# One decoder kernel on one core: the seven weight products of a pair of column blocks in another order, and two of their four weight sums made by accumulating DMAs instead of VectorE

## The chip, the cores and the metric

The kernel runs on one core of one Trainium2 chip. What counts is the device time of one execution in microseconds, the median over runs.

## What is computed

A stack of four layers and one more block over 256 tokens of width 1024, all in float32. Each layer has two feed-forward parts around an attention part; of the reference this is the part that the change touches:

```
def swiglu(x, w13, w2):
    gate, up = jnp.split(x @ w13, 2, axis=-1)
    return (jax.nn.silu(gate) * up) @ w2
...
x = layer_norm(ALPHA * x + 0.5 * swiglu(x, ffn1_w13[i], ffn1_w2[i]), ln_g[i, 0], ln_b[i, 0])
...
x = layer_norm(ALPHA * x + 0.5 * swiglu(x, ffn2_w13[i], ffn2_w2[i]), ln_g[i, 2], ln_b[i, 2])
```

`x` is 256 x 1024, `w13` is 1024 x 5632, `w2` is 2816 x 1024. There are eight such feed-forward parts.

## The kernel before

**Units.** All weights stream from HBM in units of 128 x 2048 floats (1 MB) through a ring of slots. SyncE issues the load of a unit as soon as TensorE has counted the slot's old unit as used (`unit_used`). ScalarE then makes the high part of the unit (`split_hi`, an ACTIVATE `whi<-raw` at L522), VectorE the low part (`split_lo`, a TENSOR_TENSOR `wlo<-raw,whi` at L530, written over `raw`), and each product is three matmuls, high by high, high by low, low by high (`mm3`, L690 to L692). Each engine has its own instruction stream, written out by hand; semaphores join them. An engine that waits holds back all that stands behind in its stream.

**Blocks and pairs.** The hidden width of 2816 is done in 11 blocks of 256 columns (`ffn_order`). A plain block takes two up-units (gate and up columns, each half of the 1024 inputs) and one down-unit. In six of the eight feed-forward parts the blocks 4 and 5, and 8 and 9, are taken as pairs (`PAIRED`), 12 pairs in all. A pair q, q+1 is a 2 x 2 product of blocks done with seven products in place of eight, after Strassen's scheme: sums of weight units (`form_1`, `form_2`, the sum written over `raw`, and `form_2` once more, here called the four weight sums) are multiplied with sums of the rows of x (`rows_s`, split into `rows_h` and `rows_l`), and the products are joined through PSUM banks and four SBUF tiles `term[0]` to `term[3]`.

**Names.** In a pair, v is the unit index of `up(q+1, first half)`, v+1 and v+2 are the two halves of block q, v+3 the second half of block q+1, v+4 and v+5 the down-units of blocks q-1 and q. `before_pair` is VectorE's code during block q-1 and makes the first sums; `paired` is there three times, on ScalarE, VectorE and TensorE, and is the pair itself; `product` is one of the seven products, 12 matmuls of 512 columns. `gate_rows` is the silu times up product of one half of the rows, `gturn` its transposition, `gated_low` and `gated_high` split the result for the down-product `dn`. In the trace the tiles `form_1` and `form_2` are both called `form`, and all `term` tiles `term`. GpSimd works in the feed-forward parts only on the norms around them.

## Time and profile before

| | us |
|---|---|
| median of 3 runs (lowest, highest) | 2476.29 (2475.51, 2476.77) |
| the profiled execution's own time | 2476.37 |
| its span, first to last instruction | 2474.6 |
| TensorE matmul busy | 2423.2 |
| VectorE busy | 1766.0 |
| ScalarE busy | 1255.2 |
| GpSimd busy | 423.4 |

The span is what the rows below are counted in; outside it lie 1.8 us of the profiled execution. The granted TensorE clock was 0.997 of full speed over the span. Busy TensorE is matmuls in flight, so the figure says that something was always in flight, not that the array was at its peak.

### The profile page before, as it was taken

How to read it: one execution, taken by the hardware profiler on the slowest of the kernel's cores; microseconds unless marked ns; L12 is line 12 of the kernel's file. 1: busy time of each engine (PE TensorE's matmuls, PEld its weight loads, DVE VectorE, ACT ScalarE, POOL GpSimd, SP SyncE). 2: the span in 40 equal slices, each digit the busy share in tenths (PEclk: the TensorE clock that was granted, in tenths of full speed). 3: DMA queues.
4: the chain of work that ended last, by engine and by line, in shares of the span. 5: the costliest groups of instructions: out<-in, count | busy, mean ns of one | idle time of the engine just before them, and what ended most of it. 6: DMA issues, size and time to landing. Idle time of an engine off the chain costs nothing. (4 is left out here: it accounts for less than half of the span.)

```text
span 2474.6 us, 32841 instructions
## 1 busy us (share of the span) xinstructions
PE 2423.2 (98%) x13095; PEld 2039.7 (82%) x13095; DVE 1766.0 (71%) x2348; ACT 1255.2 (51%) x1571; POOL 423.4 (17%) x463
## 2 busy tenths in 40 slices
PE   9999999999999999999989999999999998999999
PEld 7888878888888888888877888888878877998998
DVE  5466678778765787787667886887676657897554
ACT  5445555554554555545555555554553455444442
POOL 0002310000001100000231000002359702680000
PEclk9999999999999999999999999999999999999999
DMA  8555445556554455565425555555445542335553
GB/s 269 189 187 157 144 143 191 200 170 197 195 171 137 137 193 198 171 201 191 150 69 180 195 194 179 189 191 169 138 137 187 187 151 89 108 132 202 173 187 111
DMA packets 313944, 418.09 MB, mean 169 GB/s; under 512 B 18761, under 2 KB 271042, under 8 KB 313794
## 3 DMA queue, kind: packets, MB, share of 16 engines
q1 hardware_dynamic: 313794, 416.01, 51.6%
q8 instruction: 105, 1.72, 0.3%
q14 instruction: 45, 0.37, 0.0%
HBM read 414.92 MB, written 1.05 MB: 168 GB/s over the span
## 5 line engine op out<-in xcount | busy, mean ns | idle before, releaser
L530 DVE TENSOR_TENSOR wlo<-raw,whi 128x2048 fp32r<-128x2048 f32 (+1 forms) x388 | 900.5, 2341 | 155.2 <-ACT whi L522 154.5
L522 ACT ACTIVATE whi<-raw 128x2048 fp32r<-128x2048 f32 (+1 forms) x393 | 732.7, 1888 | 6.9 <-DMA raw<-in_ffn_w_dram 4.1
L690 PE MATMUL ps<-whi,xh 128*128 128x512 f32 (+2 forms) x1511 | 566.7, 375 | 7.5 <-DVE wlo L1633 2.2
L692 PE MATMUL ps<-whi,xl 128*128 128x512 f32 (+2 forms) x1511 | 559.5, 370 | 0.0
L691 PE MATMUL ps<-wlo,xh 128*128 128x512 f32 (+2 forms) x1511 | 559.3, 370 | 0.0
L690 PE MATMUL ps<-whi,oh 128*128 128x512 f32 x944 | 380.0, 403 | 0.0
L692 PE MATMUL ps<-whi,ol 128*128 128x512 f32 x944 | 369.1, 391 | 0.0
L691 PE MATMUL ps<-wlo,oh 128*128 128x512 f32 x944 | 367.9, 390 | 0.0
L690 PEld LDWEIGHTS ps<-whi,xh 128*128 128x128 f32 x1511 | 285.0, 189 | 62.0 <-issue 11.5
L692 PEld LDWEIGHTS ps<-whi,xl 128*128 128x128 f32 x1511 | 285.0, 189 | 48.8
L691 PEld LDWEIGHTS ps<-wlo,xh 128*128 128x128 f32 x1511 | 285.3, 189 | 46.4
L877 POOL TENSOR_TENSOR rstd<-ve,mhalf 128x1 f32<-128x1 f32 x26 | 18.8, 724 | 1483.8 <-DVE ve L1577 1302.5
L1076 ACT ACTIVATE sg<-ps 128x256 f32<-128x256 f32 x140 | 53.2, 380 | 321.1 <-PE ps L692 318.9
L1749 DVE TENSOR_TENSOR gt<-sg,ps 128x256 f32<-128x256 f32 x140 | 58.6, 419 | 215.1 <-ACT sg L1076 211.8
L692 PEld LDWEIGHTS ps<-whi,ol 128*128 128x128 f32 x944 | 177.1, 188 | 38.8
L690 PEld LDWEIGHTS ps<-whi,oh 128*128 128x128 f32 x944 | 177.5, 188 | 34.3 <-issue 2.1
L691 PEld LDWEIGHTS ps<-wlo,oh 128*128 128x128 f32 x944 | 177.8, 188 | 32.5
L690 PE MATMUL ps<-xh,whi 128*128 128x256 f32 (+2 forms) x496 | 138.5, 282 | 1.0 <-DVE wlo L530 1.0
L691 PE MATMUL ps<-xl,whi 128*128 128x256 f32 (+2 forms) x496 | 136.1, 277 | 0.0
L692 PE MATMUL ps<-xh,wlo 128*128 128x256 f32 (+2 forms) x496 | 136.0, 277 | 0.0
L1084 ACT ACTIVATE oh<-ps 128x512 fp32r<-128x512 f32 x88 | 52.8, 600 | 120.6 <-PE ps L2433 120.6
L690 PEld LDWEIGHTS ps<-xh,whi 128*128 128x128 f32 (+2 forms) x496 | 91.9, 185 | 3.1 <-DVE wlo L530 1.7
(413 smaller groups left out, 3543.2 us busy)
## 6 DMA issues: line engine op xcount, KB each, us to landing
raw<-in_ffn_w_dram SPq DMA_DIRECT2D x350, 512.0 KB, 4.8
raw<-in_ffn_w_dram SPq DMA_DIRECT2D x88, 1024.0 KB, 5.0
raw<-in_w_ff_dram SPq DMA_DIRECT2D x32, 1024.0 KB, 5.3
raw<-in_w_out_dram SPq DMA_DIRECT2D x20, 1024.0 KB, 4.9
raw<-in_w_in_dram SPq DMA_DIRECT2D x20, 1024.0 KB, 5.1
raw<-in_dsa_w_in_dram SPq DMA_DIRECT2D x32, 512.0 KB, 4.7
raw<-in_dsa_w_in_dram SPq DMA_DIRECT2D x12, 1024.0 KB, 5.1
raw<-in_fox_w_in_dram SPq DMA_DIRECT2D x16, 512.0 KB, 4.8
```

Source lines behind the costliest of these rows:

```text
L522: act.activation(hi(u)[:, 0:w], raw[:, (slot[u] + 1) % SLOTS, 0:w], ACT.Copy).then_inc(sem("hi_ready"), 1)
L530: dve.tensor_tensor(lo(u)[:, 0:w], raw[:, (slot[u] + 1) % SLOTS, 0:w], hi(u)[:, 0:w].bitcast(F32), ALU.subtract).then_inc(sem("lo_ready"), 1)
L690: pe.matmul(o, ah, bh, start=start, stop=False, skip_group_check=True)
L691: pe.matmul(o, ah, bl, start=False, stop=False, skip_group_check=True)
L692: return pe.matmul(o, al, bh, start=False, stop=stop, skip_group_check=True)
L877: pool.tensor_tensor(rstd[:, t, 0:1], ve[:, t, 0:1], mhalf[:, 0:1], ALU.pow).then_inc(sem("rstd_ready"), 1)
L1076: act.activation(sg[:, t, :], src, ACT.Silu).then_inc(sem("silu_done"), 1)
L1084: act.activation(oh[:, c:c + 2, :], ps[:, 6, :].rearrange("p (c s) -> p c s", c=2), ACT.Copy).then_inc(sem("gh_ready"), 1)
L1749: dve.tensor_tensor(gt[:, t, :], sg[:, t, :], up, ALU.mult).then_inc(sem("g_made"), 1)
```

## The change

The seven products are taken in another order and with other signs of the sums, so that four of them (first, third, fifth, seventh) add up in PSUM bank 5 without a reset between, and two (second, fourth) in bank 7. Two of the four weight sums per pair, the one over the raw of unit v+1 and the second one of `form_2`, are no longer made by VectorE but by DMAs with an add that GpSimd issues, from SBUF onto SBUF, 1 MB each. Both later readers (ScalarE's split of v+1, and its `form_high` of the fourth form) wait on the DMAs' semaphores `third_form` and `fourth_form`, VectorE's splits too. ScalarE now keeps four PSUM banks per pair in `term` tiles instead of two; VectorE has three additions of terms instead of five. The used-count of units v+1 and v+2 is given in one step after the fifth product, where it was given after the fourth and the fifth.

```diff
+                if kind == "ffn":
+                    A, D = ffn_units(st)
+                    for n, q in enumerate(st["pairs"]):
+                        v = A(q + 1)
+                        landed(pool, v + 2)
+                        pool.wait_ge(sem("form_made"), b("form_made", 0) + 2 * n + 1)
+                        pool.dma_start(raw_of(v + 1), raw_of(v + 2), accum_op=ALU.add).then_inc(sem("third_form"), 16)
+                        landed(pool, v + 3)
+                        pool.wait_ge(sem("form_lo"), b("form_lo", 0) + 3 * n + 2)
+                        pool.dma_start(form_2[:, :], raw_of(v + 3), accum_op=ALU.add).then_inc(sem("fourth_form"), 16)
...
                     def form_high(n, f, dst, src):
 
-                        act.wait_ge(sem("form_made"), b("form_made", 0) + 4 * n + f)
+                        if f == 3:
+                            act.wait_ge(sem("fourth_form"), b("fourth_form", 0) + 16 * n + 16)
+                        else:
+                            act.wait_ge(sem("form_made"), b("form_made", 0) + 2 * n + f)
                         act.activation(dst[:, :], src[:, :], ACT.Copy).then_inc(sem("form_hi"), 1)
 
+                    def keep(n, k, bank):
+
+                        act.activation(term[k][:, :], ps[:, bank, :], ACT.Copy).then_inc(sem("term_kept"), 1)
+
                     def paired(q):
 
                         n, v = pairs.index(q), A(q + 1)
-                        act.wait_ge(sem("form_made"), b("form_made", 0) + 4 * n + 3)
+                        act.wait_ge(sem("third_form"), b("third_form", 0) + 16 * n + 16)
                         split_hi(act, v + 2)
                         act.wait_ge(sem("unit_used"), v + 1)
-                        act.activation(term[0][:, :], ps[:, 4, :], ACT.Copy).then_inc(sem("term_kept"), 1)
+                        keep(n, 0, 5)
                         split_hi(act, v + 3)
+                        act.wait_ge(sem("form_used"), b("form_used", 0) + 3 * n + 1)
+                        keep(n, 1, 7)
                         act.wait_ge(sem("form_used"), b("form_used", 0) + 3 * n + 2)
-                        act.activation(term[1][:, :], ps[:, 7, :], ACT.Copy).then_inc(sem("term_kept"), 1)
-                        form_high(n, 4, form_4h, form_2)
+                        keep(n, 2, 5)
+                        form_high(n, 3, form_4h, form_2)
                         split_hi(act, v + 4)
+                        act.wait_ge(sem("unit_used"), v + 3)
+                        keep(n, 3, 5)
+                        act.wait_ge(sem("block_made"), b("block_made", 0) + 3 * n + 1)
+                        silu(q, 0, term[2][:, 0:256])
                         act.wait_ge(sem("block_made"), b("block_made", 0) + 3 * n + 2)
-                        silu(q, 0, term[3][:, 0:256])
                         silu(q, 1, term[1][:, 0:256])
                         split_hi(act, v + 5)
-                        act.wait_ge(sem("unit_used"), v + 4)
-                        silu(q + 1, 0, ps[:, 4, 0:256])
                         act.wait_ge(sem("block_made"), b("block_made", 0) + 3 * n + 3)
...
                         if i + 1 in pairs:
                             split_hi(act, A(i + 2))
-                            form_high(pairs.index(i + 1), 2, form_2h, form_2)
+                            form_high(pairs.index(i + 1), 1, form_1h, form_1)
...
                             silu(i, t, ps[:, 4 + t, 0:256])
+                            if t == 0 and i + 1 in pairs:
+                                form_high(pairs.index(i + 1), 2, form_2h, form_2)
...
-                        if i + 1 in pairs:
-                            form_high(pairs.index(i + 1), 1, form_1h, form_1)
-                        elif 0 < i < FIT - 1:
+                        if 0 < i < FIT - 1 and i + 1 not in pairs:
                             split_hi(act, D(i - 1) + ahead[u])
...
-                        ch.link(tt(rows_s[:, 0], first[:, :, r1], second_[:, :, r1], ALU.add))
+                        ch.link(tt(rows_s[:, 0], first[:, :, r1], second_[:, :, r1], ALU.subtract))
...
-                        tt(rows_s[:, 3], second_[:, :, r0], rows_s[:, 1], ALU.subtract).then_inc(sem("rows_made"), 1)
+                        tt(rows_s[:, 3], second_[:, :, r0], rows_s[:, 1], ALU.add).then_inc(sem("rows_made"), 1)
...
-                        n, v, made = pairs.index(q), A(q + 1), b("form_made", 0)
+                        n, v, made = pairs.index(q), A(q + 1), b("form_made", 0) + 2 * pairs.index(q)
                         landed(dve, v)
                         landed(dve, v + 1)
-                        tt(form_1[:, :], raw_of(v + 1), raw_of(v), ALU.subtract).then_inc(sem("form_made"), 1)
+                        tt(form_1[:, :], raw_of(v + 1), raw_of(v), ALU.add).then_inc(sem("form_made"), 1)
                         split_lo(dve, v)
                         landed(dve, v + 2)
-                        dve.wait_ge(sem("form_made"), made + 4 * n + 1)
-                        tt(form_2[:, :], raw_of(v + 2), form_1[:, :], ALU.subtract).then_inc(sem("form_made"), 1)
+                        dve.wait_ge(sem("form_made"), made + 1)
+                        tt(form_2[:, :], raw_of(v + 2), form_1[:, :], ALU.add).then_inc(sem("form_made"), 1)
                         gate_rows(q - 1, 0, ps[:, 4, 256:512])
-                        tt(raw_of(v + 1), raw_of(v + 2), raw_of(v + 1), ALU.subtract).then_inc(sem("form_made"), 1)
+                        form_low(n, 1, form_1l, form_1, form_1h)
                         gate_rows(q - 1, 1, ps[:, 5, 256:512])
-                        form_low(n, 1, form_2l, form_2, form_2h)
-                        form_low(n, 2, form_1l, form_1, form_1h)
+                        form_low(n, 2, form_2l, form_2, form_2h)
                         gated_low(q - 1)
 
                     def paired(q):
 
                         n, v = pairs.index(q), A(q + 1)
-                        kept, sums, blocks, use = (b(name, 0) + k * n for name, k in (("term_kept", 2), ("term_sum", 2), ("block_made", 3), ("form_used", 3)))
+                        kept, use = b("term_kept", 0) + 4 * n, b("form_used", 0) + 3 * n
+                        dve.wait_ge(sem("third_form"), b("third_form", 0) + 16 * n + 16)
                         split_lo(dve, v + 2)
-                        dve.wait_ge(sem("form_used"), use + 1)
-                        dve.wait_ge(sem("term_kept"), kept + 1)
-                        tt(term[0][:, :], term[0][:, :], ps[:, 5, :], ALU.add).then_inc(sem("term_sum"), 1)
-                        landed(dve, v + 3)
-                        tt(form_2[:, :], raw_of(v + 3), form_2[:, :], ALU.subtract).then_inc(sem("form_made"), 1)
+                        dve.wait_ge(sem("fourth_form"), b("fourth_form", 0) + 16 * n + 16)
                         split_lo(dve, v + 3)
-                        dve.wait_ge(sem("unit_used"), v + 2)
-                        dve.wait_ge(sem("term_sum"), sums + 1)
-                        tt(term[2][:, :], term[0][:, :], ps[:, 5, :], ALU.add).then_inc(sem("term_sum"), 1)
                         form_low(n, 3, form_4l, form_2, form_4h)
+                        dve.wait_ge(sem("third_done"), b("third_done", 0) + n + 1)
+                        dve.wait_ge(sem("term_kept"), kept + 3)
+                        tt(term[2][:, :], ps[:, 7, :], term[2][:, :], ALU.subtract).then_inc(sem("block_made"), 1)
                         split_lo(dve, v + 4)
-                        dve.wait_ge(sem("term_kept"), kept + 2)
-                        dve.wait_ge(sem("term_sum"), sums + 2)
-                        tt(term[1][:, :], term[1][:, :], term[2][:, :], ALU.add).then_inc(sem("block_made"), 1)
-                        dve.wait_ge(sem("unit_used"), v + 3)
-                        tt(term[3][:, :], term[0][:, :], ps[:, 7, :], ALU.add).then_inc(sem("block_made"), 1)
-                        dve.wait_ge(sem("block_made"), blocks + 2)
-                        gate_rows(q, 0, term[3][:, 256:512])
+                        dve.wait_ge(sem("term_kept"), kept + 4)
+                        tt(term[1][:, :], term[1][:, :], term[3][:, :], ALU.subtract).then_inc(sem("block_made"), 1)
+                        dve.wait_ge(sem("block_made"), b("block_made", 0) + 3 * n + 2)
+                        gate_rows(q, 0, term[2][:, 256:512])
                         gate_rows(q, 1, term[1][:, 256:512])
+                        dve.wait_ge(sem("unit_used"), v + 4)
+                        tt(term[0][:, :], term[0][:, :], ps[:, 4, :], ALU.add).then_inc(sem("block_made"), 1)
+                        split_lo(dve, v + 5)
+                        dve.wait_ge(sem("block_made"), b("block_made", 0) + 3 * n + 3)
+                        gate_rows(q + 1, 0, term[0][:, 256:512])
                         dve.wait_ge(sem("form_used"), use + 3)
-                        tt(term[2][:, :], term[2][:, :], ps[:, 5, :], ALU.add).then_inc(sem("block_made"), 1)
-                        split_lo(dve, v + 5)
-                        gate_rows(q + 1, 0, ps[:, 4, 256:512])
-                        dve.wait_ge(sem("block_made"), blocks + 3)
-                        gate_rows(q + 1, 1, term[2][:, 256:512])
+                        gate_rows(q + 1, 1, ps[:, 5, 256:512])
                         gated_low(q)
                         split_lo(dve, v + 7)
...
                         n, v = pairs.index(q), A(q + 1)
-                        low, sums, kept = b("form_lo", 0) + 3 * n, b("term_sum", 0) + 2 * n, b("term_kept", 0) + 2 * n
-                        pe.wait_ge(sem("g_made"), b("g_made", 0) + 2 * q - 1)
+                        low, kept = b("form_lo", 0) + 3 * n, b("term_kept", 0) + 4 * n
+                        pe.wait_ge(sem("g_made"), b("g_made", 0) + 2 * q)
                         unit_ready(pe, v)
-                        used(product(4, rows_of(0, 0), hi(v), lo(v), True))
-                        pe.wait_ge(sem("g_made"), b("g_made", 0) + 2 * q)
+                        used(product(5, rows_of(0, 0), hi(v), lo(v), True))
                         pe.wait_ge(sem("rows_lo"), b("rows_lo", 0) + 1)
                         pe.wait_ge(sem("form_lo"), low + 1)
-                        product(5, form_of(1), form_2h, form_2l, True).then_inc(sem("form_used"), 1)
+                        product(7, form_of(0), form_1h, form_1l, True).then_inc(sem("form_used"), 1)
                         pe.wait_ge(sem("form_lo"), low + 2)
-                        product(7, form_of(0), form_1h, form_1l, True).then_inc(sem("form_used"), 1)
-                        unit_ready(pe, v + 1)
-                        pe.wait_ge(sem("term_sum"), sums + 1)
-                        used(product(5, form_of(2), hi(v + 1), lo(v + 1), True))
+                        pe.wait_ge(sem("term_kept"), kept + 1)
+                        product(5, form_of(1), form_2h, form_2l, False).then_inc(sem("form_used"), 1)
                         unit_ready(pe, v + 2)
                         pe.wait_ge(sem("term_kept"), kept + 2)
-                        used(product(7, form_of(3), hi(v + 2), lo(v + 2), False))
+                        product(7, form_of(3), hi(v + 2), lo(v + 2), False).then_inc(sem("third_done"), 1)
+                        pe.wait_ge(sem("term_kept"), kept + 3)
+                        product(5, form_of(2), hi(v + 1), lo(v + 1), False).then_inc(sem("unit_used"), 2)
                         unit_ready(pe, v + 3)
-                        used(product(4, rows_of(1, 0), hi(v + 3), lo(v + 3), False))
+                        used(product(4, rows_of(1, 0), hi(v + 3), lo(v + 3), True))
                         pe.wait_ge(sem("form_lo"), low + 3)
-                        pe.wait_ge(sem("term_sum"), sums + 2)
-                        product(5, rows_of(1, 1), form_4h, form_4l, True).then_inc(sem("form_used"), 1)
+                        pe.wait_ge(sem("term_kept"), kept + 4)
+                        product(5, rows_of(1, 1), form_4h, form_4l, False).then_inc(sem("form_used"), 1)
                         for j in (q, q + 1):
```

In VectorE's stream, from `rows_l` on ahead of the first pair of a feed-forward part (that of pair 4, 5), before the change; a name in brackets is a semaphore that the instruction waits for, `form_54` is `form_1` and `form_57` is `form_2`:

```order
L1787 TENSOR_TENSOR form_57<-raw,form_54 128x2048 [waits form_made,loaded0]
L1749 TENSOR_TENSOR gt<-sg,ps 128x256 [waits gt_done,silu_done]
L1789 TENSOR_TENSOR raw<-raw 128x2048
L1749 TENSOR_TENSOR gt<-sg,ps 128x256 [waits silu_done]
L1761 TENSOR_TENSOR form_2l<-form_57,form_2h 128x2048 [waits form_hi]
L1761 TENSOR_TENSOR form_1l<-form_54,form_1h 128x2048 [waits form_hi]
L1755 TENSOR_TENSOR ol<-ps,oh 128x512 [waits gh_ready]
L530 TENSOR_TENSOR wlo<-raw,whi 128x2048 [waits hi_ready] x2
L1802 TENSOR_TENSOR term_65<-term_65,ps 128x512 [waits term_kept,form_used]
L1804 TENSOR_TENSOR form_57<-raw,form_57 128x2048 [waits loaded1]
L530 TENSOR_TENSOR wlo<-raw,whi 128x2048 [waits hi_ready]
L1808 TENSOR_TENSOR term_67<-term_65,ps 128x512 [waits term_sum,unit_used]
```

The same place after the change (L531 is the old L530, L1784 the old L1761):

```order
L1810 TENSOR_TENSOR form_57<-raw,form_54 128x2048 [waits form_made,loaded0]
L1772 TENSOR_TENSOR gt<-sg,ps 128x256 [waits gt_done,silu_done]
L1784 TENSOR_TENSOR form_1l<-form_54,form_1h 128x2048 [waits form_hi]
L1772 TENSOR_TENSOR gt<-sg,ps 128x256 [waits silu_done]
L1784 TENSOR_TENSOR form_2l<-form_57,form_2h 128x2048 [waits form_hi]
L1778 TENSOR_TENSOR ol<-ps,oh 128x512 [waits gh_ready]
L531 TENSOR_TENSOR wlo<-raw,whi 128x2048 [waits hi_ready,third_form]
L531 TENSOR_TENSOR wlo<-raw,whi 128x2048 [waits hi_ready]
L531 TENSOR_TENSOR wlo<-raw,whi 128x2048 [waits hi_ready,fourth_form]
L1784 TENSOR_TENSOR form_4l<-form_57,form_4h 128x2048 [waits form_hi]
L1828 TENSOR_TENSOR term_67<-ps,term_67 128x512 [waits term_kept,third_done]
```

The two big sums (L1789, L1804) are gone, `form_1l` stands where the first of them stood, and the splits of units v+1 and v+3 have the DMAs' semaphores ahead of them.

ScalarE's stream at the same place, from the split of `oh` of block q-1 on, before the change (two rows of units v+1 and v+2, then the keeping of the first product):

```order
L1084 ACTIVATE oh<-ps 128x512 [waits unit_used,gt_done]
L522 ACTIVATE whi<-raw 128x2048 [waits loaded5,form_made]
L522 ACTIVATE whi<-raw 128x2048 [waits loaded0]
L1097 ACTIVATE term_65<-ps 128x512 [waits unit_used]
L522 ACTIVATE whi<-raw 128x2048 [waits loaded1]
L1100 ACTIVATE term_66<-ps 128x512 [waits form_used]
L1089 ACTIVATE form_4h<-form_57 128x2048 [waits form_made]
L522 ACTIVATE whi<-raw 128x2048 [waits loaded2]
```

And after it:

```order
L1095 ACTIVATE oh<-ps 128x512 [waits unit_used,gt_done]
L523 ACTIVATE whi<-raw 128x2048 [waits loaded5,third_form]
L523 ACTIVATE whi<-raw 128x2048 [waits loaded0]
L1107 ACTIVATE term_65<-ps 128x512 [waits unit_used]
L523 ACTIVATE whi<-raw 128x2048 [waits loaded1]
L1107 ACTIVATE term_66<-ps 128x512 [waits form_used]
L1107 ACTIVATE term_67<-ps 128x512 [waits form_used]
L1103 ACTIVATE form_4h<-form_57 128x2048 [waits fourth_form]
L523 ACTIVATE whi<-raw 128x2048 [waits loaded2]
L1107 ACTIVATE term_68<-ps 128x512 [waits unit_used]
```

Two more keepings of a bank stand in the stream, and both waits on a DMA are ahead of work that TensorE needs.

## Rows read from the trace of the kernel before

**Rows 1.** The page: busy time by engine, DMA packets, the load queue's share.

```profile
PE 2423.2 (98%) x13095; PEld 2039.7 (82%) x13095; DVE 1766.0 (71%) x2348; ACT 1255.2 (51%) x1571; POOL 423.4 (17%) x463
DMA packets 313944, 418.09 MB, mean 169 GB/s; under 512 B 18761, under 2 KB 271042, under 8 KB 313794
q1 hardware_dynamic: 313794, 416.01, 51.6%
```

**Rows 2.** Waits of TensorE from 345 to 1800 us: total, times, longest.

```profile
PE ps L2732 <- DVE qkT L1982: 3.8, 4, 1.2
...
PE ps L690 <- DVE wlo L561: 0.7, 2, 0.4
```

**Rows 3.** Timeline of TensorE, first pair: the first matmul of some products.

```profile
405.42 0.39 PE L690 MATMUL ps<-whi,xh 128*128 128x512 f32 x1
...
408.15 0.39 PE L690 MATMUL ps<-form_2h,rows_h 128*128 128x512 f32 x1
...
410.92 0.39 PE L690 MATMUL ps<-form_1h,rows_h 128*128 128x512 f32 x1
...
419.25 0.39 PE L690 MATMUL ps<-whi,xh 128*128 128x512 f32 x1
...
421.98 0.39 PE L690 MATMUL ps<-form_4h,xh 128*128 128x512 f32 x1
...
424.70 0.39 PE L690 MATMUL ps<-whi,oh 128*128 128x512 f32 x1
...
427.43 0.60 PE L2433 MATMUL ps<-ident,gt 128*128 128x128 f32 x4
```

**Rows 4.** VectorE, by line: the sums of all 12 pairs.

```profile
L1789 DVE TENSOR_TENSOR raw<-raw x12: 2282/2285/2286, 399.4 to 1623.2; 128x2048 f32<-128x2048 f32 x12
...
L1813 DVE TENSOR_TENSOR term<-term,term x12: 684/685/687, 421.7 to 1645.7; 128x512 f32<-128x512 f32 x12
```

**Rows 5.** Timeline of VectorE around the first pair.

```profile
394.57 2.28 DVE L1787 TENSOR_TENSOR form<-raw,form 128x2048 f32<-128x2048 f32 x1
...
401.98 2.28 DVE L1761 TENSOR_TENSOR form_2l<-form,form_2h 128x2048 fp32r<-128x2048 f32 x1
...
406.99 4.48 DVE L530 TENSOR_TENSOR wlo<-raw,whi 128x2048 fp32r<-128x2048 f32 x2
```

**Rows 6.** Timeline of ScalarE in and behind the first pair.

```profile
403.37 3.71 ACT L522 ACTIVATE whi<-raw 128x2048 fp32r<-128x2048 f32 x2
408.35 0.60 ACT L1097 ACTIVATE term<-ps 128x512 f32<-128x512 f32 x1 [1.26 <-PE ps L692]
408.84 1.91 ACT L522 ACTIVATE whi<-raw 128x2048 fp32r<-128x2048 f32 x1
...
414.39 1.91 ACT L1089 ACTIVATE form_4h<-form 128x2048 fp32r<-128x2048 f32 x1
416.20 1.90 ACT L522 ACTIVATE whi<-raw 128x2048 fp32r<-128x2048 f32 x1
...
428.56 3.71 ACT L522 ACTIVATE whi<-raw 128x2048 fp32r<-128x2048 f32 x2
```

**Rows 7.** Timelines around the second pair: VectorE's second sum, and TensorE's first product.

```profile
458.93 2.29 DVE L1787 TENSOR_TENSOR form<-raw,form 128x2048 f32<-128x2048 f32 x1 [1.39 <-DMA raw<-in_ffn_w_dram]
...
470.14 0.39 PE L690 MATMUL ps<-whi,xh 128*128 128x512 f32 x1
```

**Rows 8.** DMA issues: KB each, median us from issue to landing.

```profile
raw<-in_ffn_w_dram SPq DMA_DIRECT2D x88, 1024.0 KB, 5.0
```

**Rows 9.** Timeline of SyncE's queue: issues of loads, start and length of the merged row.

```profile
377.49 17.70 SPq L503 DMA_DIRECT2D raw<-in_ffn_w_dram  x8
399.71 6.27 SPq L505 DMA_DIRECT2D raw<-in_ffn_w_dram  x2
```

**Rows 10.** Stretches: PE, PEld, DVE, ACT, POOL busy, clock, DMA share, GB/s.

```profile
404.20:417.00 12.80, 12.80 (x58) 10.44 (x57) 12.60 (x9) 8.39 (x7) 0.00 (x0) 1.00 0.45 164
458.90:471.10 12.20, 12.20 (x58) 10.07 (x57) 9.92 (x7) 7.91 (x7) 0.00 (x0) 1.00 0.52 172
```

More of the change, by code:

```diff
@@ L175, in stages_plan @@
             n = len(st["pairs"])
-            made.update(h0_done=FIT - 2 * n, rows_made=min(n, 1), rows_hi=min(n, 1), rows_lo=min(n, 1), form_made=4 * n, form_hi=3 * n,
-                        form_lo=3 * n, form_used=3 * n, term_kept=2 * n, term_sum=2 * n, block_made=3 * n)
+            made.update(h0_done=FIT - 2 * n, rows_made=min(n, 1), rows_hi=min(n, 1), rows_lo=min(n, 1), form_made=2 * n, form_hi=3 * n,
+                        form_lo=3 * n, form_used=3 * n, third_done=n, term_kept=4 * n, block_made=3 * n,
+                        third_form=16 * n, fourth_form=16 * n)
         if "lift" in st:
@@ L1108, in paired @@
-                        silu(q + 1, 0, ps[:, 4, 0:256])
                         act.wait_ge(sem("block_made"), b("block_made", 0) + 3 * n + 3)
-                        silu(q + 1, 1, term[2][:, 0:256])
+                        silu(q + 1, 0, term[0][:, 0:256])
+                        act.wait_ge(sem("form_used"), b("form_used", 0) + 3 * n + 3)
+                        silu(q + 1, 1, ps[:, 5, 0:256])
                         gated_high(q)
```

## The prediction

> **What bounds the kernel now.** I read the page first. TensorE is busy for 2423.2 us of a span of 2474.6 [rows 1], so 51 us in which nothing is in flight are all that better feeding could give back. The waits of TensorE say where they are: from 345 to 1800 us, where all 12 pairs lie, the longest is 3.8 us in total at L2732, which is attention; the largest one at a weight product is 0.7 us at L690, behind L561, a split in the attention part; none names a sum, a form or a term [rows 2]. The timeline of the first pair shows the same: seven products start one behind the other, 405.42, 408.15, 410.92, then 419.25 and 421.98, and the down-product at 424.70 [rows 3]. The pair takes 19.28 us on TensorE with no gap, and its end does not depend on any other engine. [...]
>
> **What the change removes.** Per pair two sums of 2.285 us, both of one form, and two term additions of 0.685 us leave VectorE [rows 4]: 5.94 us, for 12 pairs 71 us of its 1766.0. Nothing waits for VectorE in the pairs, so this is worth 0 us by itself. The cover is TensorE's stream; VectorE's own relief would count only where TensorE waits for it.
>
> **What stays.** TensorE does the same seven products, 84 matmuls a pair, four of them with `rows_h` and three with `xh` as before. The first product, with `xh`, took 2.73 us and the second, with `rows_h`, 2.77 [rows 3]; even if the order made all seven equally fast, that is 4 x 0.04 x 12 = 1.9 us. The order costs and gives 0.
>
> **What it adds on ScalarE.** Two more keepings of a bank of 0.60 us per pair [rows 6], 14 us of engine time. Keeping 1 must stand between the second product's end and the fourth's start, keeping 2 between the third's end and the fifth's start, keeping 3 between the fifth's end and the seventh's start; each has one product, 2.7 us, and needs 0.2 to start (408.15 to 408.35) and 0.60 to run, so up to 1.9 us of another ACTIVATE may be in its way. That is just one split of 1.9. In the present stream the splits start right behind a keeping and so end before the next. I cost them at 0 if the DMAs land in time.
>
> **The two DMAs.** This is the term that decides. The third sum (issue behind the landing of v+2 and `form_1`) can be issued in the first pair by 394.57, where `form_2` started with no wait [rows 5], and in the second at 458.93, where it had waited 1.39 us for just that landing [rows 7]. What is queued behind its wait on ScalarE: two splits (3.71 us), then keeping 0 (0.60), and for that one TensorE waits, ahead of the third product. Deadline: 410.92 - 3.71 - 0.60 - 0.20 = 406.4 [rows 3, 6], 1.0 us behind the pair's start. In the second pair the start is 470.14, so the deadline is 471.1. The budget is 11.8 us in the first pair and 12.2 in the second.
>
> The fourth sum is issued when `form_2l` is made. It stands where now the first low form does, which started at 401.98 and took 2.28 us [rows 5]: 404.3. Behind its wait on VectorE stands the split of v+3 (2.29), which the sixth product at 419.25 needs: 419.25 - 2.29 - 0.20 = 416.8. ScalarE's own deadline (`form_4h`, a split, keeping 3, before 421.98) is 421.98 - 0.60 - 1.90 - 1.91 = 417.6, later. The budget is 12.5 us. The sum of the low form behind it ends at 421.4, ahead of the seventh product at 421.98; then come a term, a split, a term and two gates (0.7 + 2.3 + 0.7 + 0.8), by 425.9, and the transposition needs them at 427.43 [rows 3].
>
> How long such a DMA takes, no row shows. Bounds: the page gives 51.6% of 16 engines over 2474.6 us for 416.01 MB [rows 1], 3.07 us of all engines per million bytes, 3.2 us per unit. A load of a unit lands 5.0 us after issue [rows 8], so 1.8 us are fixed. From below the add costs one pass, 5.0 us, as a load. From above it costs three passes (two operands read, one written, none overlapped), 9.7 + 1.8 = 11.5 us, and waits for all loads of the stretch as well, 0.52 x 12.2 = 6.3 us [rows 10]: 17.8 us. I take two passes, since a load's read and write are already one pass and the add reads twice: 6.4 + 1.8 = 8.2 us alone. Of the loads' 6.3 us it may wait for nothing or for all: 8.2 to 14.5, middle 11.4. For the fourth the stretch has 0.45 x 12.8 = 5.8 us of loads: 8.2 to 14.0, middle 11.1. Both middles are inside the budgets, by 0.4 to 0.8 us and by 1.4 us. The cover is thin: each us beyond is 12 us in the whole.
>
> [...]
>
> **Loads.** The adds push the loads back by up to 6.4 us. The load of v+3 runs while the third sum does; it was issued by 395.2 (377.49 + 17.70) and v+4's at 399.71 [rows 9]; with 5.0 us for the load and 6.4 of delay they land by 406.6 and 411.1, and are split at 408.84 and 416.20 [rows 6]. The used-count of v+1 comes one product later, at 419.25. The load that waits for it lands by 424.6 and its split is one of the two that start at 428.56: 0 us.
>
> **The sum.** 2476.37 (the profiled execution, 1.8 of it outside the span) + 0 for the products + 0 for VectorE + 0 for ScalarE + 0 for the adds, 2476.4. The median of the runs shown is 2476.29; I say 2476.5.
>
> **The rivals.**
>
> *The adds land late* (0.30). At 14.5 us the third is 2.3 to 2.7 us over its budget, the fourth 1.5 over a budget that the stall before it has lengthened, so it adds nothing: 12 x 2.5 = 30 us, 2506. It decides from 12 us on. For it speaks that two thirds of the margin is my choice of a middle; against it that the DMA engines are free for 48% of that stretch [rows 10]. What is late next is the split of v+1, keeping 0, and the third product.
>
> *The adds are far slower* (0.09). At the upper bound, 17.8 us, the stall is 5.8 us a pair: 70 us, 2546.
>
> *The fourth add waits for VectorE* (0.06). [...]
>
> *Faster* (0.05). VectorE's 71 us would have to end waits of TensorE, and in the pairs there are none. The source would be one that I do not see, 5 us or more of the 51: about 2470.
>
> *No change* has the other 0.50.
>
> **How the numbers follow.** The time is that of no change. What a measurement of this kernel can tell from no change is 0.2%, 5 us. Faster 0.05, same 0.50, slower 0.45 (0.30 + 0.09 + 0.06). No change alone would lie within 2474 to 2480. For eight in ten the range must take in the late adds and the lock: up to 2525, a stall of 4 us a pair, which leaves out the far slower adds and a little of the late ones (0.12), and down to 2473, which leaves out most of faster (0.04).
>
> **What would show it.** Right: a second DMA queue with 24 issues of 1024 KB, each landing in under 12 us; TensorE's waits name no product of the pairs; product starts 2.7 to 2.8 us apart; VectorE busy near 1695, ScalarE near 1269. Wrong by late adds: ScalarE's `whi` or `form_4h` waits for a DMA onto `raw` or `form` and TensorE idles ahead of its third or sixth product, 12 times alike. [...] What would upset all of it is a fixed cost of GpSimd's issue that is several us beyond the 1.8 of SyncE's, since the margins are under 1.5 us.

## The result

| | before | after |
|---|---|---|
| median, us (lowest to highest, runs) | 2475.90 (2475.28 to 2476.77, 4) | 2508.34 (2504.07 to 2513.87, 4) |
| profiled execution, its span | 2476.37, 2474.6 | 2512.1, 2510.3 |
| granted TensorE clock, mean | 0.997 | 0.993 |

The ratio is 1.0132, 95% interval 1.012 to 1.0145: 32.4 us slower. The forecast was no change, 2476.5. The time lies in the range, 2473 to 2525, and next to what the rival of the late adds gave, 2506. Of the four runs two lie at 2504 and two, with the profiled one, at 2512 to 2514; what follows is read from one of the longer two. Below, S is the start of a pair's first product, and "S+1.1" is 1.1 us behind it.

The page of the profile after, the lines that answer to [rows 1]:

```profile
PE 2435.0 (97%) x13095; PEld 2043.0 (81%) x13095; DVE 1701.1 (68%) x2300; ACT 1270.5 (51%) x1595; POOL 444.5 (18%) x487
DMA packets 317401, 443.27 MB, mean 177 GB/s; under 512 B 19145, under 2 KB 271426, under 8 KB 314178
q1 hardware_dynamic: 313794, 416.01, 51.2%
q0 software_dynamic: 3456, 25.17, 4.9%
```

VectorE lost 65 us (71 in the forecast) and ScalarE gained 15 (14), and neither is what counts. TensorE's waits from 345 to 1800 us, total, times, longest:

```profile
PE ps L691 <- DVE wlo L531: 22.4, 12, 2.9
PE ps L2748 <- DVE qkT L1999: 3.8, 4, 1.2
...
PE ps L691 <- ACT term L1107: 1.3, 2, 0.7
```

The first and the third row are new against [rows 2]: 12 waits, one a pair, for a split by VectorE, and two for a keeping. VectorE, ScalarE and GpSimd say what is behind them, in the waits of all engines in the same stretch:

```profile
POOL form L903 <- issue: 113.0, 10, 12.1
...
DVE wlo L531 <- DMA form<-raw: 75.4, 12, 7.3
...
ACT form_4h L1103 <- DMA form<-raw: 53.2, 12, 5.5
...
ACT whi L523 <- DMA raw<-raw: 33.9, 12, 4.0
...
POOL form L903 <- DMA raw<-in_ffn_w_dram: 22.1, 2, 11.2
```

`form<-raw` is the fourth add, `raw<-raw` the third. The timelines of VectorE, TensorE and GpSimd in the first pair (S = 404.60) put them in order:

```profile
399.65 2.28 DVE L1784 TENSOR_TENSOR form_2l<-form,form_2h 128x2048 fp32r<-128x2048 f32 x1
...
417.94 2.29 DVE L531 TENSOR_TENSOR wlo<-raw,whi 128x2048 fp32r<-128x2048 f32 x1 [4.81 <-DMA form<-raw]
```

```profile
410.96 0.47 PE L691 MATMUL ps<-form_2h,rows_h 128*128 128x512 f32 x1 [0.69 <-ACT term L1107]
...
420.29 0.50 PE L691 MATMUL ps<-whi,xh 128*128 128x512 f32 x1 [0.77 <-DVE wlo L531]
```

```profile
393.77 1.05 POOL L900 DMA_DIRECT2D raw<-raw  x1 [43.63 <-DMA raw<-in_ffn_w_dram]
406.86 0.90 POOL L903 DMA_DIRECT2D form<-raw  x1 [12.04 <-issue]
```

The sixth product waits for the split of unit v+3, which stands in VectorE's stream behind the wait for the fourth add. And `form_2l` is ready at 401.93, but GpSimd issues the fourth add at 406.86, S+2.3. In ten pairs GpSimd stands before this issue with nothing to wait for that the profile shows (`issue`), and goes on 0.3 us after the third add has landed. The 113.0 us of that row are its idle time since the third issue, and most of them are no fault of the hold: with the larger size below (`ring1024`) the time before the twelve fourth issues is 79.1 + 31.2 = 110.3 us, here 113.0 + 22.1 = 135.1. By line, duration of the issue and, at the end, landing; first the third add, then the fourth:

```profile
L900 POOL DMA_DIRECT2D raw<-raw x12: 860/894/1048, 393.8 to 1649.9; - x12
...
DMA to landing us min/median/max: 10.5/11.6/12.8
```

```profile
L903 POOL DMA_DIRECT2D form<-raw x12: 860/876/904, 406.9 to 1661.8; - x12
...
DMA to landing us min/median/max: 11.0/12.5/13.5
```

Over the 12 pairs the fourth add is issued at S+0.8 to S+2.3 (median S+1.1) and lands at S+12.3 to S+14.5, where the prediction's deadline is S+11.4. The pairs lose 0.95 to 4.39 us each, 35.5 us together; the whole span lost 35.7. Of that, 23.7 are the two new waits above. Another 8 are the clock. At five of the stalls, with waits of 1.9 to 2.5 us, the granted clock falls to 0.50 of full speed for 3.41 us each (not at the longest wait, 2.9 us, nor at one of 2.2); here in the third pair (TensorE idle 2.43 us before 609.47), stretches with PE, PEld, DVE, ACT, POOL busy, clock, DMA share and GB/s:

```profile
605.00:609.00 4.00, 2.04 (x9) 1.31 (x7) 1.88 (x1) 1.88 (x2) 0.00 (x0) 1.00 0.55 177
609.30:612.60 3.30, 3.13 (x7) 2.48 (x8) 3.30 (x4) 2.36 (x3) 0.00 (x0) 0.50 1.02 357
613.00:617.00 4.00, 4.00 (x20) 3.29 (x19) 3.47 (x5) 1.95 (x2) 0.00 (x0) 1.00 0.78 249
```

The sixth product there takes 4.3 to 4.45 us against 2.84 to 2.88 in the seven other pairs, 1.6 us five times. The last 4 us are 0.3 at each of 14 restarts: the first matmul after a wait runs 0.47 to 0.51 us instead of 0.39 at full clock, and the idle time shown is a little shorter than the delay.

### The profile page after: what moved, and what is told of

It is laid out like the page before. It is cut to its first block and busy times, and to the rows that moved or that the text cites. A ratio compares the mean times of both kernels' runs of the same rounds, so it can differ in the third digit from the quotient of the medians.

```text
span 2510.3 us, 32877 instructions
## 1 busy us (share of the span) xinstructions
PE 2435.0 (97%) x13095; PEld 2043.0 (81%) x13095; DVE 1701.1 (68%) x2300; ACT 1270.5 (51%) x1595; POOL 444.5 (18%) x487
## 5 line engine op out<-in xcount | busy, mean ns | idle before, releaser
L531 DVE TENSOR_TENSOR wlo<-raw,whi 128x2048 fp32r<-128x2048 f32 (+1 forms) x388 | 900.5, 2341 | 284.2 <-ACT whi L523 207.9
L691 PE MATMUL ps<-whi,xh 128*128 128x512 f32 (+2 forms) x1511 | 571.1, 378 | 29.9 <-DVE wlo L531 22.4
L900 POOL DMA_DIRECT2D raw<-raw x12 | 10.8, 904 | 591.1 <-DMA raw<-in_ffn_w_dram 591.1
## 6 DMA issues: line engine op xcount, KB each, us to landing
raw<-raw POOLq DMA_DIRECT2D x12, 1024.0 KB, 11.6
```

The costliest lines, as they stand in the source:

```text
L531: dve.tensor_tensor(lo(u)[:, 0:w], raw[:, (slot[u] + 1) % SLOTS, 0:w], hi(u)[:, 0:w].bitcast(F32), ALU.subtract).then_inc(sem("lo_ready"), 1)
L691: pe.matmul(o, ah, bh, start=start, stop=False, skip_group_check=True)
L900: pool.dma_start(raw_of(v + 1), raw_of(v + 2), accum_op=ALU.add).then_inc(sem("third_form"), 16)
```

## The experiments

The runs stand in three groups; each group ran on one chip with runs of the kernel before beside it (medians 2475.76, 2475.58, 2475.61). Ratios are against those. "The ring", and "space" in it, are names of the recorded expectations for a theory: that a number with which the kernel is built, `dynamic_dma_scratch_size`, decides whether the fourth add has to wait for the landing of the third. `ring1024` and `ring576` change that number.

### What each part costs alone

**All sums on VectorE, only the new order (`order_only`).** The diff shows the sums alone: with the third sum back in its old place VectorE makes `form_2l` ahead of `form_1l` again, here and in `fourth_only`, and TensorE waits for both.

```diff
-                        pool.dma_start(raw_of(v + 1), raw_of(v + 2), accum_op=ALU.add).then_inc(sem("third_form"), 16)
-                        pool.dma_start(form_2[:, :], raw_of(v + 3), accum_op=ALU.add).then_inc(sem("fourth_form"), 16)
...
+                        tt(raw_of(v + 1), raw_of(v + 2), raw_of(v + 1), ALU.add).then_inc(sem("third_form"), 16)
...
+                        tt(form_2[:, :], raw_of(v + 3), form_2[:, :], ALU.add).then_inc(sem("fourth_form"), 16)
```

> The new order of the products with all four weight sums on VectorE, no DMA from GpSimd. Both theories: no add, no stall, 2476 us as before. Rival: the new order itself (two more keepings, one bank for four products, the used-count of v+1 given late) costs a part: 2480 or more, with waits of TensorE for a term.

Measured: 2475.49 us, ratio 0.9999 (0.9989 to 1.0008), no loss in any pair. Order and extra keepings are free.

**Only the third sum as a DMA (`third_only`):** the second `tt` above in place of its DMA.

> The changed kernel, but the fourth weight sum is made by VectorE again (2.29 us, between the splits of v+2 and v+3). Theory, the ring: the whole loss comes from the fourth add, what is left is the third add's own lateness of up to 0.9 us in a few pairs: 2477 to 2481 us. Rival, bandwidth or late third add: the third add still pushes back ScalarE's splits and the loads and half of the loss stays, about 2490.

Measured: 2476.15 us, 1.0002 (0.9992 to 1.0011). The add lands 9.3/11.5/13.2 us after its issue, at S-1.6 to S+2.2; the only losses are 1.15 us in the first pair and 0.29 in the tenth, for keeping 0. So the third add is as slow here as in the changed kernel, and nearly harmless; the time is a little below the 2477 to 2481 expected.

**Only the fourth as a DMA (`fourth_only`):** the first `tt` above in place of its DMA.

> The changed kernel, but the third weight sum is made by VectorE (2.29 us, where the kernel before made it), so that the fourth add has the queue to itself. It is issued about 1.1 us ahead of the pair's first product. Theory, the ring: it takes 10 to 12.5 us, lands 9 to 11.4 us into the pair, around the deadline of 11.5, and costs 0 to 0.5 us a pair: 2476 to 2482 us. Rival, bandwidth: it lands as late as now, 13.5 us into the pair, about 2500 us.

Measured: 2475.58 us, 0.9999 (0.999 to 1.0009), no loss. By line:

```profile
L900 POOL DMA_DIRECT2D form<-raw x12: 868/900/1048, 403.3 to 1627.2; - x12
its engine sat idle before it (us, times) until:
  DVE form_2l L1781: 697.3, 12
...
DMA to landing us min/median/max: 8.3/8.3/9.0
```

Without the other add it is issued when `form_2l` is made, S-2.0, and takes 8.3 us (10 to 12.5 were expected), with VectorE at work beside it. So its cost is not a property of the instruction; both adds together make the loss.

### Is it the hold before the fourth issue?

The changed kernel, like the one before, is built with `dynamic_dma_scratch_size=512`. Two kernels have 1024 and 576 in its place; in the one with 1024 the matrix `ones` also shares a tile with `gt`. The runs show what the number does to the issue of the fourth add, and nothing else of it is used here.

```diff
-    nc = _bacc.Bacc("TRN2", target_bir_lowering=False, num_devices=1, dynamic_dma_scratch_size=512)
+    nc = _bacc.Bacc("TRN2", target_bir_lowering=False, num_devices=1, dynamic_dma_scratch_size=1024)
...
-        ones = sb("ones", [P, P])
+        ones = gt[:, 0, 0:P]
```

> [...] Theory, the ring: the second add waits for space and so for the landing of the first; with space it is issued when form_2l is made, some 2.7 us ahead of the pair's first product in place of 1.1 behind it, its packets follow those of the first add, it lands 9 to 10 us into the pair, before the deadline at 11.5, and only the two late third sums are left: 2478 to 2482 us. Rival, bandwidth: the adds and loads together are too much for the DMA engines; the second add's landing hardly moves and the time stays at 2500 to 2510. Rival, one add at a time whatever the ring: the issue stays 0.2 to 0.3 us behind the first landing, 2508.

Measured: 2484.42 us, 1.0037 (1.0024 to 1.005). The fourth add by line:

```profile
L903 POOL DMA_DIRECT2D form<-raw x12: 856/863/904, 403.7 to 1634.3; - x12
its engine sat idle before it (us, times) until:
  DMA raw<-in_ffn_w_dram: 79.1, 8
  DVE form_2l L1784: 31.2, 4
...
DMA to landing us min/median/max: 9.9/11.1/13.4
```

No `issue` row is left. In five pairs the fourth starts at S-2.0, lands at S+8.1 to S+8.9 and costs nothing. In most of the others it now waits for the landing of v+3, a load that the third add has pushed back, starts at S-0.2 to S+0.4, and lands up to S+13.8. The time is above the 2478 to 2482 of the theory and far below both rivals.

With 576 (`ring576`: the same line, and nothing else):

> [...]

Measured: 2482.47 us, 1.0033 (1.0021 to 1.0045). In six pairs the fourth starts at S-2.0 with the third still in flight. No `issue` row is left here either: six fourth issues wait for v+3 (62.4 us), six for `form_2l` (47.2). So the fourth add is held with 512, in ten pairs of twelve, and with 576 in none. The hold is a cause: without it three quarters of the loss go. In the five pairs where `ring1024` issues at S-2.0, the changed kernel issues at S+0.9 to S+1.3, some 3 us later.

**Is lateness alone enough (`fourth_late`)?** `fourth_only` with one wait more, so that the fourth add starts as late as in the changed kernel, or later:

```diff
+                        pool.wait_ge(sem("hi_ready"), v + 3)
                         pool.dma_start(form_2[:, :], raw_of(v + 3), accum_op=ALU.add).then_inc(sem("fourth_form"), 16)
```

> The kernel of fourth_only (third sum on VectorE, only the fourth by a DMA), with GpSimd made to wait until ScalarE has split unit v+2, so that the add is issued about 1.9 us into the pair in place of 2.0 ahead of it. Theory, lateness: there is no third add here, and still the loss comes back: the add now starts beside the load of v+5, takes 11 to 12 us, lands 13 to 14 us in, stalls the sixth product by 1.5 to 2.5 us: 2495 to 2508 us. Rival, two adds are too much together: with one add alone the time stays under 2480.

Measured: 2475.58 us, 0.9999 (0.999 to 1.0009). Issued at S+2.3, it lands 8.3 us later (8.3/8.3/8.8), at S+10.6, in time. The first theory, that the late issue is enough, falls. The add must also take 12.5 us. Here the load of v+5 is not pushed back by a third add and lands at S+5.0. The packets tell the loads apart: a down-unit such as v+4 or v+5 comes in 256 packets of 4096 B, an up-unit such as v+3 or v+6 in 1024 of 1024 B. Among the add's packets run at most 18 of v+5 and 170 to 245 of v+6, which is issued at S+2.9. In the changed kernel it is 23 to 82 of the large ones and 710 to 920 of v+6.

### What makes an add long?

**Plain copies in place of both adds (`copies`).**

```diff
-                        pool.dma_start(raw_of(v + 1), raw_of(v + 2), accum_op=ALU.add).then_inc(sem("third_form"), 16)
+                        pool.dma_start(raw_of(v + 1), raw_of(v + 2)).then_inc(sem("third_form"), 16)
...
-                        pool.dma_start(form_2[:, :], raw_of(v + 3), accum_op=ALU.add).then_inc(sem("fourth_form"), 16)
+                        pool.dma_start(form_2[:, :], raw_of(v + 3)).then_inc(sem("fourth_form"), 16)
```

> The changed kernel with plain copies from SBUF to SBUF in place of the two adds (the additions of the two weight sums are left out). If the second read is what makes an 8 KB packet take 628 ns in place of 2 x 159, the copy's take 320 to 340 ns, each DMA lands about 2.5 us sooner, the second one 11 us into the pair or earlier, and the time is 2476 to 2482. If the issue from GpSimd and the queueing behind loads are the cost and the add is not, both land as now: 2500 to 2508.

Measured: 2475.04 us, 0.9999 (0.9989 to 1.0009). The copies land after 7.2 us (third) and 5.7 us (fourth), medians. A packet of 8192 B takes 309 ns as a copy and 628 ns as an add, medians, a ratio of 2.03; shared alike, the 128 packets of an add are eight for each of the 16 DMA engines of the page, 5.0 us. The third copy lands at S-4.3 to S-2.7, so the fourth is issued at S-2.0 in all but the first pair (S-1.4): with copies both the hold and the late landing are gone, and this run does not part them. The ratio fits the two passes that the prediction took for an add and one for a load, which was its author's estimate.

**The third add with the load of v+3 held until it has landed (`third_quiet`, on `third_only`):** in SyncE's loop over the loads, `held_loads` gives for each unit v+3 the count of `third_form`:

```diff
+                if u in held_loads:
+                    sp.wait_ge(sem("third_form"), held_loads[u])
                 load(sp, u, units[u])
```

> The kernel of third_only (fourth sum on VectorE), with SyncE's load of v+3 held until the third add has landed. Theory, queueing behind the load: the add has the engines nearly to itself until the load of v+4, and lands 8 to 9 us after issue in place of 11.5, some 3 us ahead of the pair's first product; the load of v+3 lands within 2.5 us of the pair's start, in time: 2475 to 2478 us. Rival: GpSimd's own preparation is what takes the first 4 to 5 us, and the add still needs 11 us.

Measured: 2476.04 us, 1.0002 (0.9993 to 1.0012). The add lands after 7.0/7.0/8.7 us instead of 9.3/11.5/13.2; its first packet comes 1.5 us after the issue, against 2.5 to 5.0 in the changed kernel, where 390 to 920 of the 1024 packets of the load of v+3 (median 890) pass ahead of it.

### The load that meets the fourth add

In the changed kernel the load of v+5 is issued at S+0.2 and lands at S+7.0 to S+9.1; the fourth add is issued at S+1.1. Three kernels move loads, both adds kept and `dynamic_dma_scratch_size` at 512. `v5_held` holds the load of v+5 until the fourth add has landed, `v3_held` that of v+3 until the third has, `both_held` does both. SyncE issues the loads in order, so each hold also holds those behind it: `v3_held` that of v+4, and `v5_held` that of v+6, issued at S+2.9 in the changed kernel and at S+7.9 to S+9.0 in `v5_held`.

```diff
+                if u in held_loads:
+                    sp.wait_ge(sem(held_loads[u][0]), held_loads[u][1])
                 load(sp, u, units[u])
```

> The changed kernel with one wait more: SyncE issues the load of unit v+5 of each pair only when the fourth add has landed (in the changed kernel it issues it 0.2 us behind the pair's start S, and its packets mix with the fourth add's). The load is split only some 18 us behind S. Theory (the fourth add is late because it starts at S+1.1, held until the third has landed, and then shares the DMA engines with the load of v+5): alone it takes 8.3 to 9 us, so it lands at S+9.4 to S+10.5 in most pairs, inside the deadline S+11.5; the sixth product waits in at most two or three pairs, in-pair loss 0 to 8 us, 2476 to 2485 us, add's landing 8.3 to 9.5 us after its issue. Rival A (the hold alone makes it late, or what is left of v+4's load from S-0.8 to S+3.8 lengthens it): lands 11 to 12 us after its issue, S+12 to S+13, loss 1 to 2 us a pair, 2490 to 2505. Rival B (the held load is itself late next: v+6 and the down-units behind it on SyncE's queue): the adds land in time but TensorE waits for a split of v+5 or a later unit, 2480 to 2510, with DVE wlo or ACT whi behind DMA raw in the waits behind the pair.

Measured: 2476.02 us, 1.0004 (0.9995 to 1.0013). The whole loss is gone but 0.13 us in one pair. The timeline of GpSimd in the first pair, and the fourth add by line:

```profile
394.13 1.05 POOL L907 DMA_DIRECT2D raw<-raw  x1 [43.34 <-DMA raw<-in_ffn_w_dram]
406.32 0.90 POOL L910 DMA_DIRECT2D form<-raw  x1 [11.13 <-DMA raw<-in_ffn_w_dram]
```

```profile
L910 POOL DMA_DIRECT2D form<-raw x12: 860/878/904, 406.3 to 1629.9; - x12
its engine sat idle before it (us, times) until:
  issue: 88.6, 8
  DMA raw<-in_ffn_w_dram: 43.7, 4
...
DMA to landing us min/median/max: 7.0/7.0/7.1
```

Up to the issue little differs from the changed kernel: the third add is nearly as late (S-1.1 to S+1.2, there S-0.3 to S+2.0), the hold is there (`issue`, 8 times), the fourth is issued at S+0.4 to S+1.5. Only then it takes 7.0 us instead of 12.5 (8.3 to 9 were expected) and lands at S+7.5 to S+8.6. Its first packet comes 1.4 to 1.5 us after the issue and its packets take 5.2 us, against 3.4 (2.1 to 4.1) and 8.8 (7.5 to 9.7) in the changed kernel. At most two load packets run among them, for 740 to 970, nine tenths of them and more from v+6. In the changed kernel the last 4 to 26 of the add's 128 packets (eight for each engine, shared alike) start only behind S+10; in `fourth_late`, with a later issue, none does. So what this run takes away is the load of v+5 and all behind it. Which of the two, v+5 or v+6, makes the add long, no run parts. For v+5 speaks `fourth_late`: there v+6 is free to run and v+5 is nearly through, and the add takes 8.3 us.

> The changed kernel with SyncE's load of unit v+3 held until the third add has landed; both adds are in. The third add then lands in 7.1 us, S-3.8 (as in the run with the third add alone and the same hold), so the ring is free early, but GpSimd's own wait for the landing of v+3 (S+1.2) sets the fourth's issue, and the loads of v+4 and v+5 stand behind it. Theory: the fourth starts at S+1.3 as in the changed kernel and meets the packets of v+4 and v+5: lands 11.5 to 13 us later, S+12.8 to S+14, no gain over the changed kernel: 2495 to 2510 us, third product never late. Rival (what makes the fourth long is the third add's own packets or the backlog it leaves, not the loads beside the fourth): 8.3 to 9.5 us, S+10 to S+10.8, no stall, 2475 to 2480.

Measured: 2501.91 us, 1.0105 (1.009 to 1.0121). The third add lands at S-4.1 to S-2.1 (median S-3.8), some 6 us ahead of the fourth issue, and there is no `issue` row. But the load of v+3 now lands late, GpSimd waits for it (`DMA raw<-in_ffn_w_dram: 148.2, 12`), and the fourth starts at S+2.0 to S+3.7. Its first packet comes 3.4 to 4.9 us later, behind packets of v+4 and v+5, so the third add's own packets are not needed to make it long. The profiled execution is the slowest of the four, 2509.09:

```profile
L910 POOL DMA_DIRECT2D form<-raw x12: 860/876/904, 408.1 to 1662.8; - x12
...
DMA to landing us min/median/max: 10.1/10.9/12.5
```

> Both holds in the changed kernel: the load of v+3 until the third add has landed, the load of v+5 until the fourth has. Theory (each add is in time when no load runs beside it, though the fourth still starts only behind the landing of v+3 at S+1.2): third lands at S-3.8, fourth 8.3 to 9.5 us after S+1.3, S+9.6 to S+10.8; no stall in any pair, 2475 to 2478 us, the same as before. Rival (the loads of the stretch have to be moved anyway and come late when both are held: the split of v+3, v+4 or v+5 is late next): adds land in time but TensorE waits for a split, 2480 to 2510.

Measured: 2475.34 us, 0.9999 (0.999 to 1.0008), no loss. The adds land after 6.9/7.0/8.7 and 6.9/7.5/8.7 us; the fourth at S+8.9 to S+10.9, although it starts as late as in `v3_held`. With v+3 held the hold on v+5 and what follows it decides between 1.0105 and 0.9999; without it, between 1.0132 and 1.0004.

## Why the prediction was wrong in its mechanism, though the time lies in its range

The forecast was no change, and the kernel is 1.3% slower, clear of the noise. That the time lies in the range is no merit of the mechanism: the range was drawn up to 2525 to take in rivals, and the one that gives this size has the stall at another product.

- **TensorE's stream, the order, VectorE's relief, the two keepings: 0.** Right: `order_only` is at 0.9999. The 65 us that VectorE lost gave nothing.
- **The third add: middle 11.4 us against a budget of 11.8 and 12.2.** Right: 11.6, and only two pairs waited, 0.7 us at most. The "8.2 alone" was 1.2 too long: 7.0 with no load beside it (`third_quiet`, `v5_held`); the 8.3 of `fourth_only` has some 40 load packets of 4096 B among its own. The bounds of 5.0 and 17.8 held. Most of the load of v+3 went ahead of the add, in eight of the twelve pairs 840 to 920 of its 1024 packets.
- **"The fourth sum is issued when `form_2l` is made", 404.3, with a budget of 12.5 us.** This is the step that failed. It took GpSimd's second DMA to be free of its first. With `dynamic_dma_scratch_size=512` the second is held until the first has landed, in ten pairs of twelve: S+1.1 in place of S-1.1 (404.3 against 405.42), and S-2.0 is what five and six pairs of the kernels with a larger number show. Of the 12.5 us of the budget 10.3 were left. The page of the profile and all rows of before could not show it, since no DMA ran on this queue; the number, though, stands in the kernel, and the prediction did not ask what it bears on.
- **The fourth's duration, middle 11.1 us.** It took 12.5, since an add that starts at S+1.1 behind a third add meets other loads than one that starts ahead of the pair: in the pairs of `ring1024` and `ring576` that start at S-2.0 it takes 10.2 to 11.1, as forecast. The loads were spread over a stretch as an average share; what counts is which load is in flight at that time. The load of v+5 with those behind it is the difference between 7.0 and 12.5. That of v+5 would be through at S+5.0, as in `fourth_late`; the third add pushes v+3 and v+4 back, v+4 to a landing at S+2.6 to S+3.8, and so v+5 to S+7.0 to S+9.1, into the fourth add.
- **The sum of both:** 1.1 + 12.5 is 13.6, 2.2 us past S+11.4; the mean wait was 22.4 / 12 = 1.9. Each wait then costs 0.3 at the restart, and the clock the rest of the 3.0 a pair. One of the two errors alone is harmless: late and quiet (`fourth_late`, `v5_held`) is in time, early and beside loads (five and six pairs of `ring1024` and `ring576`, landing by S+9.1) as well.
- **The rival of the late adds, 2506.** Right in size and wrong in place, which is luck: it put the stall at the third product, and said that the fourth "adds nothing" to it. It is the sixth, behind the fourth add. Its condition ("from 12 us on") was set for the third add; the fourth met it, with 12.5. Its 2.5 us a pair has no term for the restart or the clock.
- **The rival in which the fourth add waits for VectorE ("the lock").** Its 0.06 and its share in the range rest on a wait that no run shows: in `fourth_only` the add's first packet came 1.4 to 1.6 us after the issue, while VectorE worked on (in the first pair from 402.58 to 409.86 without a pause, with the issue at 403.3).
- **Loads.** That they are pushed back by the adds and still are split in time is right for VectorE and ScalarE. But the load of v+3 is also waited for by GpSimd, ahead of the fourth add, which the prediction had not put on the path. With 1024 and 576 that is most of what is left of the loss.
- **The clock.** The prediction had no term for it: 8 of the 35.5 us are matmuls at a granted clock of 0.50 behind waits of 1.9 to 2.5 us.

What stays open: how the 5.5 us come about by which the fourth add is longer in the changed kernel than in `v5_held`. In the trace 1.9 are the later first packet and 3.6 the longer stretch of its packets, of which the last few start late; the trace does not name the engines. Why those are late, and whether v+5 or v+6 delays them, no run here shows: a hold on v+6 alone was not tried. None of these kernels is faster than the kernel before, for VectorE's relief has nothing to buy here; versions that would use it for more pairs were not tried.

## What to carry to other kernels

When work moves to a DMA queue that was empty before, ask two things that the old profile can't show as an average: whether a second such transfer is issued while the first is in flight (here with 576, but not with 512), and which transfer will be in flight at that time. Give each DMA a start, an end and a deadline on one time axis, with the loads that it meets. If it comes late, a wait that moves a load with slack out of its way may be all that is needed: here one wait on SyncE gave back nearly all of the 32 us, and it held more than the one load that it named.

## What was not expected of the hardware

- A second accumulating DMA of 1 MB on GpSimd's queue is held until the first has landed when the kernel is built with `dynamic_dma_scratch_size=512` (the issue comes 0.3 us behind that landing in ten pairs of twelve), not with 576 or 1024. The profile names no cause for it but `issue`.
- An add's first packet comes 1.5 us after the issue with quiet engines and 2.5 to 5.0 us behind a full load of 1 MB; in eight of the twelve pairs 840 to 920 of that load's 1024 packets went ahead of it.
- A wait of TensorE of 1.9 to 2.5 us was followed by 3.41 us at a granted clock of 0.50 in five pairs of twelve, 1.6 us more each time. One wait of 2.2 and one of 2.9 us were not.
